# A two-block transformer kernel: latent products split in three, first gate tiles entered together, and five waits moved

## What is computed

```python
for i in range(2):                                   # first block: two layers
    proj = x @ w_in[i]                               # q, k, v, latents, rope, gates
    o_na = neighborhood_attention(q_na, k_na, v_na, na_rpb[i])       # bias table + mask
    q_mla = rms_norm(q_lat, q_norm_g[i]) @ w_uq[i]   # 256x768 @ 768x768
    kv    = rms_norm(kv_lat, kv_norm_g[i]) @ w_ukv[i]  # 256x256 @ 256x1024
    ...                                              # rope, latent attention
    merged = sigmoid(g_na) * (o_na @ w_na_o[i]) + sigmoid(g_mla) * (o_mla @ w_mla_o[i])
    x = layer_norm(ALPHA * x + merged @ w_out[i])
    f = swiglu(x, ...) if i == 0 else moe_swiglu(x, ...)   # 2816 wide; 8 experts, top 2, 3584 wide
    x = layer_norm(ALPHA * x + f + sigmoid(x @ w_ple_gate[i]) * (p[i] @ w_ple[i]))
# second block: one hybrid layer
groups = rms_norm(four kinds of mixers(rms_norm(x) @ w_in))
x = x + groups @ w_out
h2 = rms_norm(x, g_ffn)
return x + (silu(h2 @ w_gate) * (h2 @ w_up)) @ w_down      # 2816 wide
```

## Time and profile before

| | us |
|---|---|
| median of three runs | 2080.58 |
| lowest and highest | 2076.1, 2080.73 |
| the profiled execution | 2080.06 |
| its span, first to last record | 2078.1 |
| PE busy | 2025.6 (97%) |
| DVE busy | 1516.2 (73%) |
| ACT busy | 989.0 (48%) |
| POOL busy | 76.8 (4%) |

### The profile page before, as it was taken

The page is one execution under the profiler, slowest core; times in us unless marked ns, Lnnn a source line. Parts: engine busy times, 40 slices in busy tenths (PEclk is TensorE's granted clock), DMA queues, the critical chain, the costliest instruction groups (busy, mean ns, idle before and its releaser), DMA issues.

```text
span 2078.1 us, 28424 instructions
## 1 busy us (share of the span) xinstructions
PE 2025.6 (97%) x11434; PEld 1735.3 (84%) x11434; DVE 1516.2 (73%) x1485; ACT 989.0 (48%) x1034; POOL 76.8 (4%) x43
## 2 busy tenths in 40 slices
PE   8999999999999989999999999999999989989998
PEld 8888799989888778888888888888888878768998
DVE  3564677765463698888888888898888966646775
ACT  0164110011253277877778787877777744531000
POOL 1011100000001200000000000000000000100000
PEclk9999999999999999999999999999999999999999
DMA  9543589753633579999999999999999964415550
GB/s 318 189 154 107 162 290 317 264 172 97 212 122 119 230 295 382 381 382 368 386 384 379 385 376 386 370 381 382 377 384 393 384 219 127 154 52 188 175 183 21
DMA packets 180972, 553.28 MB, mean 266 GB/s; under 512 B 9248, under 2 KB 107168, under 8 KB 137488
## 3 DMA queue, kind: packets, MB, share of 16 engines
q1 hardware_dynamic: 172048, 517.55, 67.8%
q10 hardware_dynamic: 6912, 25.02, 3.0%
q0 software_dynamic: 1920, 9.40, 1.2%
HBM read 528.09 MB, written 23.59 MB: 265 GB/s over the span
## 4 chain that ended last, share of the span: by engine, by line
PE 94%; DVE 3%; ACT 2%; issue 1%; DMA 0%; DVEq 0%; ACTq 0%; SPq 0%
PE act_ps L1084 29%; PE dve_ps L1109 15%; PE act_ps L961 14%; PE dve_ps L858 7%; PE dve_ps L961 7%; PE act_ps L858 3%; PE job_ps L1045 3%; PE job_ps L1037 3%; PE act_ps L1004 2%; PE job_ps L984 2%; PE job_ps L1092 1%; PE act_ps L1208 1%; PE job_ps L908 1%; PE job_ps L927 1%; PE job_ps L939 1%
## 5 line engine op out<-in xcount | busy, mean ns | idle before, releaser
L2167 DVE TENSOR_TENSOR weights_rest<-weight_ring,expert_short 128x2048 fp32r<-128x2048 f32 x336 | 762.7, 2289 | 104.9 <-ACT expert_short L1589 104.3
L1589 ACT ACTIVATE expert_short<-weight_ring 128x2048 fp32r<-128x2048 f32 x336 | 640.5, 1917 | 102.2 <-PE act_ps L1084 66.7
L1084 PE MATMUL act_ps<-expert_short,tokens_short 128*128 128x512 f32 x896 | 354.4, 396 | 4.9 <-ACT arena_o L1606 2.5
L1084 PE MATMUL act_ps<-expert_short,tokens_rest 128*128 128x512 f32 x896 | 349.4, 390 | 0.0
L1084 PE MATMUL act_ps<-weights_rest,tokens_short 128*128 128x512 f32 x896 | 349.3, 390 | 0.0
L1501 ACT ACTIVATE arena_mla<-act_ps 128x256 f32<-128x256 f32 (+1 forms) x72 | 31.0, 431 | 391.5 <-PE act_ps L961 323.6
L1084 PEld LDWEIGHTS act_ps<-expert_short,tokens_short 128*128 128x128 f32 x896 | 168.3, 188 | 39.6 <-issue 4.7
L1084 PEld LDWEIGHTS act_ps<-expert_short,tokens_rest 128*128 128x128 f32 x896 | 168.3, 188 | 36.1
L1084 PEld LDWEIGHTS act_ps<-weights_rest,tokens_short 128*128 128x128 f32 x896 | 168.5, 188 | 33.4
L2096 DVE TENSOR_TENSOR weights_rest<-weight_ring,ffn_weights_short 128x2048 fp32r<-128x2048 f32 x66 | 151.3, 2292 | 2.3
L1109 PE MATMUL dve_ps<-expert_short,hidden_short 128*128 128x512 f32 x448 | 139.6, 393 | 0.0
(11 more groups left out here) (360 smaller groups left out, 3641.7 us busy)
## 6 DMA issues: line engine op xcount, KB each, us to landing
weight_ring<-in_moe_w SPq DMA_DIRECT2D x336, 1024.0 KB, 7.0
weight_ring<-in_w_in SPq DMA_DIRECT2D x45, 1024.0 KB, 8.0
weight_ring<-in_ffn_w SPq DMA_DIRECT2D x32, 1024.0 KB, 7.2
weight_ring<-in_w_out SPq DMA_DIRECT2D x12, 1024.0 KB, 7.0
weight_ring<-in_w_gate SPq DMA_DIRECT2D x11, 1024.0 KB, 5.4
weight_ring<-in_w_up SPq DMA_DIRECT2D x11, 1024.0 KB, 8.2
weight_ring<-in_w_down SPq DMA_DIRECT2D x10, 1024.0 KB, 7.1
weight_ring<-in_w_ple_gate SPq DMA_DIRECT2D x8, 1024.0 KB, 6.2
```

The costliest lines, as they stand in the source:

```text
L1084: m = nc.tensor.matmul(bank[0:CAP, :], a[:, 4 * c + k, :], w[:, k, :], start=(c == k == i == 0), stop=(c == 1 and k == 3 and i == 2))
L1589: nc.scalar.activation(shorts[u % SHORTS][:, :], ring[:, slot, half], ACT.Copy).then_inc(moe_w_short, 1)
L2167: V.tensor_tensor(ring_lo[slot][:, half], ring[:, slot, half], shorts[u % SHORTS][:, :], ALU.subtract)\
```

## The change

**Latent products.** They become split products. `w_uq` becomes three units of six k-steps by 256 columns (1536 columns each), `w_ukv` one unit of 2048; a layer has 18 input units instead of 14, and the gates are 10 to 17. The normed latents are cut too, into `latents_short` and `latents_rest` (`lat_x`) on DVE. The short parts of units 6 to 11 are made by ACT (`in_short`), between its reads, and their rests by DVE (`in_rest`); the first two gate units, 10 and 11, thereby lose their casts on DVE. A new counter, `values_unit_used`, lets unit 6 be cut when the first value unit is done.

**Waits and order.** POOL's first `mask_bias` waits for the first six units to be cut. Its clearing of `clear_rows` waits until the FFN's input is cut. At the experts' entry, the fourth short is made before `z_summed` is awaited and the third rest before the last `embedded_gated`; two short buffers trade places; a one-column silu stands at the head of each expert's loop. The last FFN's input: the mixed squares come in five steps (`LAST_STEPS`), DVE folds the squares of tiles 0 to 3 into one, PE sums five instead of eight, ACT makes the eight casts, and PE runs ten 512-column products whose result is overwritten (`idle_products`) before it takes both first gate tiles k by k (`first_gate_tiles`). The last sums are added and stored in five steps, each bank when its own sum is done.

Not shown: semaphores, buffers, DMA panels, and unit shapes in `split_product`.

```diff
@@ constants @@
+LAST_STEPS = ((0, 2), (2, 4), (4, 6), (6, 7), (7, 8))
@@ buffers @@
+lat_x = [parts("latents_short", "arena_o", [P, DT, SEQ]), parts("latents_rest", "probs", [P, DT, SEQ])]
@@ in_units @@
-block, c = queries_at[l] + (0, 1, 3, 7, 8, 9, 10)[i // 2], i % 2
-a, d = tiles_before[block]
-used = c + 1 if i in (4, 5) else 2 * (c + 1)
-units.append((block, c, (dve_tile_ready, d + used) if i in (2, 3) else (act_tile_ready, a + used)))
+at = (0, 0, 1, 1, 3, 3, 4, 4, 5, 6, 7, 7, 8, 8, 9, 9, 10, 10)[i]
+c = i % 2 if i not in (8, 9) else 0
+a, d = tiles_before[queries_at[l] + at]
+used = (act_tile_ready, a + 2 * (c + 1))
+if i in (2, 3):
+    used = dve_tile_ready, d + 2 * (c + 1)
+elif i == 4:
+    used = values_unit_used, l + 1
+elif i == 5:
+    used = act_tile_ready, a + 2
+units.append((queries_at[l] + at, c, used))
@@ SP: end of the program @@
-for b in range(4):
-    sp.wait_ge(out_ready, b + 1)
-    sp.dma_start(out_rows[:, 2 * b:2 * b + 2, :], x[:, 2 * b:2 * b + 2, :]).then_inc(out_stored, 16)
-sp.wait_ge(out_stored, 16 * 4)
+for i, (j0, j1) in enumerate(LAST_STEPS):
+    sp.wait_ge(out_ready, i + 1)
+    sp.dma_start(out_rows[:, j0:j1, :], x[:, j0:j1, :]).then_inc(out_stored, 16)
+sp.wait_ge(out_stored, 16 * len(LAST_STEPS))
@@ POOL: before the layers @@
+pool.wait_ge(in_w_split, 6)
@@ POOL: end of a layer @@
+pool.wait_ge(ffn_x_split, DT)
@@ PE: new helper @@
+def idle_products(bank, a, count):
+    for _ in range(count):
+        nc.tensor.matmul(bank[:, :], a[:, 0:P], a[:, 0:512], start=True, stop=True)
+def first_gate_tiles(w, after):
+    pe.wait_ge(act_tile_done, n.a - 1)
+    idle_products(act_ps[n.a % 2], ff_w[0], 10)
+    banks = [act_bank(), act_bank()]
+    for k in range(DT):
+        pe.wait_ge(*after(k))
+        for j, bank in enumerate(banks):
+            for i, (a, x_part) in enumerate(((w[0], 0), (w[0], 1), (w[1], 0))):
+                m = nc.tensor.matmul(bank[:, 0:SEQ], a[:, k, j * P:(j + 1) * P], ff_x[x_part][:, k, :],
+                                     start=(k == i == 0), stop=(k == DT - 1 and i == 2))
+            if k == DT - 1:
+                m.then_inc(act_tile_ready, 1)
@@ PE: swiglu @@
+    if 2 * pair + 2 == f_tiles and j % 2 and j < DT - 1:
+        m.then_inc(last_sums, 1)
+if u == 0 and after:
+    first_gate_tiles((short, rest), after)
+    continue
-    m = split_product(bank[:, 0:SEQ], (short, rest), at, ff_x, after if u == j == 0 else None)
+    m = split_product(bank[:, 0:SEQ], (short, rest), at, ff_x)
@@ PE: latent products @@
+    if c == 0:
+        m.then_inc(values_unit_used, 1)
-for _ in range(2):
-    feature_tiles("A", weights(QLT, 384), k_tiles(lat, QLT))
-w = weights(KVLT, D)
-kv = [lat[:, QLT + i, :] for i in range(KVLT)]
+for i in (6, 7, 8):
+    w = in_weights(i)
+    for j in range(2):
+        split_product(act_bank()[:, 0:SEQ], w, slice(j * P, (j + 1) * P), lat_x).then_inc(act_tile_ready, 1)
+w = in_weights(9)
+n.block += 3
-    product(dve_bank()[:, 0:SEQ], cols(w, j * P, (j + 1) * P), kv).then_inc(dve_tile_ready, 1)
+    split_product(dve_bank()[:, 0:SEQ], w, slice(j * P, (j + 1) * P), lat_x, first_k=QLT).then_inc(dve_tile_ready, 1)
-    product(act_bank()[:, :], [a[:, i * P:(i + 1) * P] for a in kv], cols(w, D // 2, D)).then_inc(act_tile_ready, 1)
+    bank = act_bank()
+    for k in range(KVLT):
+        for p, (a, part) in enumerate(((w[0], 0), (w[0], 1), (w[1], 0))):
+            m = nc.tensor.matmul(bank[:, :], lat_x[part][:, QLT + k, i * P:(i + 1) * P], a[:, k, D // 2:D],
+                                 start=(k == p == 0), stop=(k == KVLT - 1 and p == 2))
+    m.then_inc(act_tile_ready, 1)
@@ PE: sum of squares before the last FFN @@
-norm_sum(const("ones"), zs, lambda k: (x_mixed_squared, k // 2 + 1))
+mixed_squares = [(x_folded, 1), (x_mixed_squared, 3), (x_mixed_squared, 3), (x_mixed_squared, 4), (x_mixed_squared, 5)]
+norm_sum(const("ones"), [zs[0]] + zs[4:], lambda k: mixed_squares[k])
@@ ACT: experts, one() @@
+nc.scalar.activation(silu_table[:, 0:1], const("one"), ACT.Silu)
@@ ACT: layer @@
+def in_short(i):
+    block, c, _ = in_units(l)[i]
+    width = QLT * 256 if i in (6, 7, 8) else 2048
+    act.wait_ge(*weights_landed(block))
+    act.wait_ge(*in_units(l)[i - 2][2])
+    nc.scalar.activation(in_w[i % 2][:, 0:width], ring[:, block % RING, c * 2048:c * 2048 + width], ACT.Copy)\
+        .then_inc(lat_w_short, 1)
+in_short(6)
+in_short(7)
+in_short(8)
+    if j % 2:
+        in_short(9 + j // 2)
+in_short(11)
-            block, c, _ = in_units(l)[6 + p + 2]
+            block, c, _ = in_units(l)[FIRST_GATE + p + 2]
@@ ACT: entry of the experts @@
+act.wait_ge(rows_sent, 16 * 2 * QT)
+expert_short(0, 3, free=False)
-act.wait_ge(rows_sent, 16 * 2 * QT)
-for u in (3, 4, 5):
+for u in (4, 5):
@@ ACT: entry of the last FFN @@
-for b in range(4):
-    act.wait_ge(x_mixed, b + 1)
-    square(z[:, 2 * b:2 * b + 2, :], x[:, 2 * b:2 * b + 2, :], x_mixed_squared)
+for i, (j0, j1) in enumerate(LAST_STEPS):
+    act.wait_ge(x_mixed, i + 1)
+    square(z[:, j0:j1, :], x[:, j0:j1, :], x_mixed_squared)
+for j in range(DT):
+    act.wait_ge(rms_ready, DT + j + 1)
+    nc.scalar.activation(ff_x[0][:, j, :], z[:, j, :], ACT.Copy).then_inc(ffn_x_short, 1)
@@ DVE: helpers @@
-    dve.wait_ge(in_w_short, 8 * l + i + 1)
+    dve.wait_ge(in_w_short, 6 * l + i + 1)
+def in_rest(l, i):
+    block, c, _ = in_units(l)[i]
+    width = QLT * 256 if i in (6, 7, 8) else 2048
+    half = slice(c * 2048, c * 2048 + width)
+    dve.wait_ge(lat_w_short, 6 * l + i - 5)
+    V.tensor_tensor(ring_lo[block % RING][:, half], ring[:, block % RING, half], in_w[i % 2][:, 0:width], ALU.subtract)\
+        .then_inc(in_w_split, 1)
-    block, c, _ = in_units(l)[6 + p]
+    block, c, _ = in_units(l)[FIRST_GATE + p]
@@ DVE: experts @@
-for u in range(0 if turn else 2, SHORTS):
+for u in range(0 if turn else 3, SHORTS):
...
@@ DVE: layer @@
-m.then_inc(latents_ready, 1)
-for i in (6, 7):
-    split_in_w(l, i)
+step(m)
+V.tensor_copy(lat_x[0][:, :, :], lat[:, :, :]).then_inc(lat_short_ready, 1)
+in_rest(l, 6)
+dve.wait_ge(lat_short_ready, l + 1)
+V.tensor_tensor(lat_x[1][:, :, :], lat[:, :, :], lat_x[0][:, :, :], ALU.subtract).then_inc(latents_ready, 1)
+for i in (7, 8, 9):
+    in_rest(l, i)
+in_rest(l, 10)
-attention(layer_pairs * l, layer_pairs, fill=lambda p: gate_rest(l, p + 1) if 1 <= p < layer_pairs - 1 else None)
+attention(layer_pairs * l, layer_pairs, fill=lambda p: in_rest(l, 11) if p == 0 else gate_rest(l, p + 1) if p < layer_pairs - 1 else None)
@@ DVE: entry of the experts @@
+expert_rest(0, 2)
@@ DVE: entry of the last FFN and end @@
-for b in range(4):
-    dve.wait_ge(mix_ready, b + 1)
-    V.tensor_tensor(x[:, 2 * b:2 * b + 2, :], x[:, 2 * b:2 * b + 2, :], tiles(mix_ps[b][:, :], 2), ALU.add)\
+for i, (j0, j1) in enumerate(LAST_STEPS):
+    dve.wait_ge(mix_ready, j0 // 2 + 1)
+    V.tensor_tensor(x[:, j0:j1, :], x[:, j0:j1, :], tiles(mix_ps[j0 // 2][:, :], 2)[:, j0 % 2:j0 % 2 + j1 - j0, :], ALU.add)\
-dve.wait_ge(x_mixed, 4)
+    if i == 1:
+        dve.wait_ge(x_mixed_squared, 2)
+        step(V.tensor_tensor(z[:, 0:2, :], z[:, 0:2, :], z[:, 2:4, :], ALU.add))
+        V.tensor_tensor(z[:, 0, :], z[:, 0, :], z[:, 1, :], ALU.add).then_inc(x_folded, 1)
+dve.wait_ge(x_mixed, len(LAST_STEPS))
-    if 1 <= j <= DT:
-        dve.wait_ge(rms_ready, DT + j)
-        V.tensor_copy(ff_x[0][:, j - 1, :], z[:, j - 1, :]).then_inc(ffn_x_short, 1)
-dve.wait_ge(down_used, total.w)
-for b in range(4):
-    V.tensor_tensor(x[:, 2 * b:2 * b + 2, :], x[:, 2 * b:2 * b + 2, :], tiles(acc_ps[b][:, :], 2), ALU.add)\
+for i, (j0, j1) in enumerate(LAST_STEPS):
+    dve.wait_ge(*((last_sums, i + 1) if j0 < DT - 2 else (down_used, total.w)))
+    V.tensor_tensor(x[:, j0:j1, :], x[:, j0:j1, :], tiles(acc_ps[j0 // 2][:, :], 2)[:, j0 % 2:j0 % 2 + j1 - j0, :], ALU.add)\
```

33 lines of the change are left out of this document (21 added, 12 removed).

## The result

| us | before | after |
|---|---|---|
| median of the runs beside each other | 2079.15 (4 runs) | 2056.43 (4 runs) |
| lowest and highest | 2076.1, 2080.73 | 2055.25, 2060.94 |
| the profiled execution | 2080.06 | 2055.25 |
| its span | 2078.1 | 2053.3 |
| mean granted clock in it | 0.992 | 0.998 |

The ratio of the times is 0.9899, with a 95% interval of 0.9886 to 0.9911: 1.0% faster, 22.7 us in the medians. The forecast was 2064.6 us (15.8 less than the profiled execution, put on the scale of the medians), in a range from 2060.5 to 2071.0.

A forecast was written before the change was run, and what follows sets the result against it. PE's own work, 94% of the span, bounds the kernel. Terms -2.74 + 1.0 - 6.45 - 0.45 - 5.4 - 1.8 = -15.8 from 2080.06 give 2064.2, stated as 2064.6 us on the medians' scale; range 2060.5 to 2071.

The forecast's parts named there:

- The mask: Layer 0: holding POOL's sum until six units are cut closes PE's wait behind a slowed DVE cast, -2.74 us.
- the collision with the normings: Layer 0: POOL's moved sum blocks DVE's normings of the latents, so PE waits for the cut latents, +1.0 us.
- Rival C: Layer 0: the port rule doesn't reach DVE's normings, so POOL doesn't block them; -1.0 us, to 2063.6; chance 0.09.
- The latents: Split latent products in both layers: gross -3.78 us a layer, less 0.55 for PE's wait at unit 9; -6.45 for both.
- Rival A: Latent products: the chains cutting units 7 and 8, at worst 6, also make PE wait; +2.2 to +4.4 us; chance 0.13.
- The experts' entry: Entry of the experts: one table load goes, the 0.8 us gap closes, the silu comes some 0.5 us sooner; -0.45 us.
- The last FFN's entry: Fewer squares (-1.0), idle products filling PE's gap and both first tiles taken k by k; -5.4 us in all.
- Rival B: Last FFN's entry: the clock halves anyway, +3.4 us, to 2068; chance 0.13 together with the change not doing what it says.
- The end: Behind PE's last product: only two one-tile sums remain and the last store is half as large; -1.8 us (-1.5 to -2.1).
- rival C with the units hidden: Latents in both layers: POOL doesn't block the normings and no cut unit makes PE wait; forecast at 2061 us.
- the low end: Whole kernel: normings unblocked, units hidden, and the better ends of the experts' and the tail's terms; 2060.5 us.
- stretches at half clock elsewhere: Stretches that come and go by themselves: a little in the range's high end; half of one profiled stretch would cost 1.7 us.

The follow-up runs named there:

- the changed kernel's second run: The changed kernel run again with no edit, beside the kernel before at 2078.4 us: median 2057.11 us (2055.33 to 2057.46).
- the two ends: The kernel before with only the new entry of the last FFN and the five steps of last sums and stores: median 2070.25 us, against 2078.2 beside it.
- the mask held: The kernel before with only POOL's first mask sum held until six units are cut: median 2074.7 us (10 runs), against 2078.2 beside it.
- the last version: The changed kernel with POOL's mask after five units and overwritten fp32 products, 2 at 455, 3 at 1684, 3 at 1786: median 2056.33 us.

## Why the prediction was wrong, and where it was right

**The edits, one by one.** The signs were as forecast, the mechanism was right but for parts of the latents and of the experts' entry, and the sum was -17.0 against -15.8. The terms that were mis-sized:

- The mask: -2.97 for the gap (2.74 forecast), and the collision with the normings +0.6 instead of +1.0. Rival C is refuted: the first norming, which began 3.3 us after POOL's sum had begun, took 3.78 us instead of 0.47 and ended 0.3 us behind it. The Trainium skill says this of operations with two SBUF inputs ("SBUF — State Buffer", "Who interferes with whom"), and the runs agree. With the mask free there was no wait, with the mask one unit earlier it blocked another operation instead. The price was smaller since the chain behind POOL's end took 8.2 us (69.48 to 77.67), not the 8.6 that I had added up.
- The latents: -5.8 instead of -6.45. The queries came out as added up, 13.5 and 13.4 us (77.72 to 91.21 in layer 0) against 12.96 + 0.55, though the wait ahead of unit 9 was only 0.3 of it and the rest lay at the starts and ends of the units. What the sum did not have: the key tiles took 3.18 us, not 2.88, and the small products behind them 1.0 instead of 0.86. PE's list shows no wait for a bank there; where these 0.4 us come from was not followed. Rival A, that units 7 and 8 wait too, did not happen.
- The experts' entry: -0.96 instead of -0.45. I had the 0.8 gap closing and the silu some 0.5 us sooner; the traces show 0.83 down to 0.29 and 2.49 down to 2.06, with the 1.1 us wait behind them unchanged. The load that went is worth its full 1.3 us here, less 0.4 for the moved work. The load took 1.28 us again, with the next operation 0.02 behind it; the 1.38 us of drain that the Trainium skill adds ("ScalarE: Activation LUTs", "What ACT_TABLE_LOAD costs") show in none of these traces, and taking one load away moved the work behind it by 1.3 us, not 2.7.
- The last FFN's entry: -5.28, forecast -5.4. Of it 1.0 are the fewer squares, 0.4 the earlier first input, and 3.85 the 48 products. These last have two reasons, told apart by runs: the clock (2.7 us, by the idle products) and the interleaving (1.8 us); they overlap, since together they would be 4.5. Rival B is refuted in all ten profiles that had the products.
- The end: -2.61 instead of -1.8. The last sums came to 0.75 us as taken (0.8), but the stores of one tile, half as large, landed 1.8 us after their issue instead of the 2.5 of those before (medians of the profile).

Two sums of the range also do not come out of their terms: rival C with the units hidden is 2064.6 - 1.0 - 1.1 = 2062.5, not 2061, and the low end with the better ends of the experts and the tail is 2061.1, not 2060.5. Neither would have reached 2056.4.

**The step that failed** was that on stretches at half clock elsewhere. I had put them at up to 1.7 us either way, as "a little" at the range's end. In the two profiles everything that the change leaves alone is 6.8 us apart, and 1.0 us at the start besides. Two errors lie in it. I took the profiled execution of before as the level to subtract from, though its 30.6 us of half clock were as much an accident as a property: the same kernel's second profile had 17 and a span 6.1 us shorter. On the medians that level was 1.4 us too high beside the result (2080.6 against 2079.15) and 2.2 beside the changed kernel's second run (2078.4). With the edits' measured sum those two levels give 2062.1 and 2061.4, still in the range; the other 4.3 to 5.7 us are the clock's. And I counted only the one stretch that the change aimed at, not that a further gap which it closes, the mask's, is one place fewer where half clock can follow.

**What the medians say.** Taken one by one against the runs beside them: the two ends -8.0, the mask -3.5, the latents -7.1 (taken out of the changed kernel). With -1.0 for the experts' entry that is -19.6; the whole is -21.3 to -22.7. By the traces the same parts come to -7.9, -3.0, -5.2 and -1.0, that is -17. (The 95% interval of the whole ratio is 2.6 us wide to either side, so that 19.6 and 21.3 are not told apart.) The rest of 4 to 6 us goes with the mean granted clock: 0.993 in the executions of the kernel before, 0.998 in those of the changed kernel. Of that difference the entry of the last FFN is 6.8 us of half clock, always there before (in each of its profiles, and already in the -17 with 2.7 us), and another part are the stretches behind the mask's gap: 3.4 us at 57 and 6.8 us at 56, in two of the four profiles that had this gap.

**What stays open.** These two don't account for all of it: 0.005 of the clock are some 20 us of half clock, of which they explain about 10 (6.8, and half of the time 3.4 to 6.8). At all other places the change made no difference that the profiles show. Half clock there lasted 23.8, 6.8, 17.0 and 20.4 us in the kernel before, its repeat, the two ends alone and the mask held (17.0 in the mean), and 6.8, 10.2, 13.6, 23.8, 23.8, 10.2, 23.8 and 13.6 us in the eight profiles of the changed kernel and its variants without fillers (15.7). Those variants had mean clocks of 0.994 to 0.998. That the unaltered one had 0.998 in 7 of 8 may be its fortune or follow from how its gaps lie to each other; the runs don't tell. As far as it is fortune, so is that part of the 22.7 us.

## What to carry to other kernels

When PE is busy for 97% of a span, compare two profiles at fixed places of its timeline and set the granted clock beside each; what differs in untouched work is the clock, and must be neither credited to the change nor subtracted from its forecast. A forecast should start from several executions' level, not from the one that was profiled, and its range should hold the spread of half-clock stretches: here 10 us between executions of one unaltered kernel. A gap of 3 us ahead of a long dense stage is worth filling with products that compute nothing where half clock follows it in every profile, as at the last FFN, and if they fit in the gap and start at once; in the three other gaps that were filled in the last version they brought nothing that the median shows. A wait that vanishes from a list is saved only if what it waited for came earlier, and not if PE was merely slower ahead of it. And a wait that moves one engine's work should be placed by what that work will block next, which here was one counter value earlier (0.7 us in the trace).

## What the runs showed of the hardware

- The same idle time of PE is followed by half clock in one execution and not in the next. The gap of 3.0 us in the hybrid layer (1799 before) was followed by 3.4 us of it in the first profile of the kernel before and by none in its second. The stretches seen lasted 3.4, 6.8 or 10.2 us, and one of 3.4 costs 1.2 to 1.7 us of PE's work. Ten overwritten products in the gap ahead of the last FFN kept the clock at 1.00 in ten profiles of ten, where it fell to 0.50 in four of four without them.
- POOL's sum kept off a DVE cast (5.59 and 5.69 us instead of 1.22) and the normings (5.76 instead of 2.46) until it ended, in each of the five arrangements, and the sum itself lasted 8.96 and 8.99 us when a subtraction had begun first, 6.7 to 6.8 otherwise.
- Behind the experts' loop PE began independent products 2.6 us after its last one, with no wait shown.
